# Hybrid decoder step on one core: gate units before attention-branch units, low parts of y in pairs, first state-space branch unit by halves

## The chip, the cores and the metric

One Trainium2 chip, one of its cores. The metric is the device time of one execution in microseconds (us). Every time below comes from the runs of the kernel before or from one profiled execution of it.

## What is computed

One layer of a decoder, for 512 prompt rows and 8 sample rows (together R = 520 columns once the input is transposed). The input is RMS-normalised and multiplied by one large matrix `w_in`. Two branches work on the result: a state-space branch (convolution, chunked scan, gated group norm, giving y with 2048 channels) and an attention branch (three head groups merged into o with 512 channels). Cut to what the change touches, the end of the layer is:

```python
y = yg.reshape(b, t, D_SSD) * ssd_norm_w          # state-space result, 2048 channels
br_ssd = y @ w_ssd_br                             # items "bs"
br_att = o @ w_att_br                             # items "ba"
mix = sigmoid(g_ssd) * br_ssd + sigmoid(g_att) * br_att   # g_ssd: items "gs", g_att: items "ga"
out = x + mix @ w_out                             # items "wo"
```

For the 8 sample rows the state-space branch is one recurrence step: each of 16 units reads a state of 128 x 8 x 128 numbers from memory, forms its share of y from it, scales it by a decay, adds an outer product and stores it again.

## The kernel before, in words

**Numbers.** Every matrix product is made in three passes of a rounded 32-bit type: each operand is split into a high part (H) and a low part (L), and wH·xH, wH·xL and wL·xH are added up in a PSUM bank. ScalarE (ACT) casts to the high part (L1136), VectorE (DVE) subtracts to get the low part (L1511 for weights, L1925 and L1928 for y, L1932 for mix).

**Items and units.** The weights come in 63 items, in the order of `weight_items`; each fills one of two slots of `w_raw`, `wH`, `wL`. SyncE (SP) issues the load of item i once item i-2 is split (L955), ACT casts it once the products of item i-2 are done (L1177), DVE then subtracts. A unit is one block of 128 output channels: a unit of gs or ga has 48 matmuls of 260 columns (8 input tiles, 3 products, 2 halves of the columns), a unit of ba 24, a unit of bs 96 (16 input tiles). gs and ga have 4 items of 2 units each, ba has 2 items of 4 units, bs has 8 items of 1 unit. Units take two pairs of PSUM banks in turn (`cm_bank`), so a unit can start only when the unit two before it has been read out: gs and ga are read by ACT (tanh, L1272), ba and bs by DVE (L1622), wo by DVE (L1639).

**The plan.** `plan()` (L95) writes one list of steps, and each engine walks the same list and does its own part of each step, strictly in order. After the scan of the prompt rows the list `rest` (L220 to L223) has 19 beats, one unit each, with the recurrence of the sample rows laid beside it:

- `sread` u (beat u, u = 0 to 15): DVE waits for the state (L1894), multiplies it with a spread copy of C in a PSUM bank (L1898, twice) and sums (L1905). GpSimd (POOL) forms the outer product (L1116), adds it to the decayed state (L1121) and issues the store (L1123).
- `sdecay` u (beat u+1): ACT scales the state by its decay, 8 instructions (L1429), once DVE has read it (L1426).
- `sload` u (beat u+2): SP waits until the slot's last store has landed (L1000) and issues the next load (L1001). There are 5 slots. SP's queue also holds the weight loads, and behind each of these, up to that of the first bs item, a copy of at most 2 MB from an input cache to an output cache (L949).
- `sgroup` g: TensorE (PE) spreads B and C of a group over the partitions, 32 small matmuls (L920); the C banks are free again only when DVE has read the group's fourth unit (L1902). `sbcopy` g: ACT copies B out of PSUM (L1420), which the outer products wait for (L1113).
- `parts` u: ACT casts unit u of y to yH (L1436), DVE subtracts to yL (L1925). yH lies where the input xH lay, so the first cast waits for the last ga unit (L1434).
- `sfinal` 0 to 2 (beats of the last three ba units): the sample rows' y, its norm and scale. PE's part is a small sum over channels (L927). `sampleparts` splits the sample columns of y.

In the order before, the beats are gs 2 (second unit), gs 3, ga 0, ga 1, ba 0, ga 2, ga 3, ba 1. The parts come four per beat in the last four beats in which the list has room for them, beats 14 to 17 (after the last ga unit and the first three ba 1 units). The first bs unit walks the 16 input tiles in order, three products at each, both halves of the columns side by side, and waits for the low part of each tile and for the sample columns' low part ahead of its first matmul (L610 to L613).

Of the kernel before, what the change touches and what calls it, by code (L numbers as in the profile page):

```python
# [25 lines left out]
P = 128  # L26
# [4 lines left out]
HALF = R // 2  # L31
# [5 lines left out]
UNITS = DSSD // P  # L37
# [24 lines left out]
def weight_items():  # L62

    items = [("rm", g, s, half) for g in range(NG) for s in "qkv" for half in range(2)]
    items += [("za", 0), ("za", 1), ("dt", 0)]
    for g in range(GROUPS):
        items.append(("bc", g))
        for j in range(2 * g, 2 * g + 2):
            items += [("x", j), ("z", j)]
    items += [("gs", j) for j in range(4)]  # L70
    for j in range(2):
        items += [("ga", 2 * j), ("ga", 2 * j + 1), ("ba", j)]
    items += [("bs", j) for j in range(KD)]
    items += [("wo", j) for j in range(4)]
    return items
# [19 lines left out]
def plan():  # L95


    out = [("squares",), ("split", 0), ("init",)]
# [15 lines left out]
    for g in range(NG):  # L114
# [13 lines left out]
        else:  # L128
            beside = []
            for unit in range(2):  # L130
                za_uses.append(proj("za", 0, unit=unit))
                _, i, units = out.pop()
# [26 lines left out]
    n, piece = B * NG, pieces()  # L159
# [27 lines left out]
    for g in range(GROUPS):  # L187
        u = PER_GROUP * g
# [29 lines left out]
    use = proj("gs", 2, unit=0)  # L218
    out += [("sprep",), ("sgroup", 0), use]
    rest = [("gs", 2, 1), ("gs", 3, 0), ("gs", 3, 1)]  # L220
    for j in range(2):
        rest += [("ga", 2 * j + half, unit) for half in range(2) for unit in range(2)]
        rest += [("ba", j, unit) for unit in range(4)]  # L223
    for beat, (kind, j, unit) in enumerate(rest):
        use = proj(kind, j, unit=unit)
        if beat < UNITS:
            if beat and beat % PER_GROUP == 0:
                out.append(("sgroup", beat // PER_GROUP))
            out.append(("sread", beat))
        if beat % PER_GROUP == 1 and beat < UNITS:  # L230
            out.append(("sbcopy", beat // PER_GROUP))
        if 0 < beat <= UNITS:
            out.append(("sdecay", beat - 1))
        if SLOTS_S <= beat - 2 < UNITS:
            out.append(("sload", beat - 2))
        if kind == "ba" and j == 1 and unit > 0:
            out.append(("sfinal", unit - 1))
        out.append(use)
        left = len(rest) - 1 - beat
        if left <= 4:  # L240
            out += [("parts", u) for u in range(4 * (4 - left), 4 * (5 - left)) if u < UNITS]
    out += [("sload", UNITS - 1)] if len(rest) - 2 < UNITS else []
    out.append(("sampleparts",))
    for j in range(KD):
# [74 lines left out]
def hybrid_kernel(nc, xT, wpack, params, consts, sel_in, state_conv, ssm_in, caches,  # L319
                  y_out, tail_out, ssmp_out, kvp_out, ssms_out, kvs_out):  # L320
    ctx = ExitStack()
    with ctx:
# [11 lines left out]
        wH = sb("wH", [P, 2, SLOT], F32R)  # L334
        wL = sb("wL", [P, 2, SLOT], F32R)
# [138 lines left out]
        yL = nc.alloc_sbuf_tensor_at("yL", [P, UNITS, R], F32R, offset=base)  # L474
        yH = nc.alloc_sbuf_tensor_at("yH", [P, UNITS, R], F32R, offset=xH_at)
# [30 lines left out]
        S = {n: sem("s_" + n) for n in names}  # L506
        ends = {}
# [11 lines left out]
        def cm_bank(i, s, hf):  # L519
            if ITEMS[i] == ("za", 0):  # L520

                return banks[((2, 3), (5, 7))[s][hf]]
            return banks[2 * (CMU[i, s] % 2) + hf]

        def wslot(w, i):
            k, n = SHAPES.get(ITEMS[i][0], (KD, 2 * P))
            return w[:, i % 2, 0:k * n].rearrange("p (k n) -> p k n", k=k)
# [36 lines left out]
        def _(pe):  # L564
# [12 lines left out]
            def proj_rows(i, g, s, half):  # L577
# [17 lines left out]
                        mm.then_inc(S["half_item_used"], 1)  # L595
                ends[i] = (banks[NT].filled, banks[NT].uses["rm", g, s, NT]) if half else (S["half_item_used"], i // 2 + 1)

            def proj_cols(i, units, tile, kind, j):

                srcH, srcL = {"bs": (yH, yL), "ba": (oH, oL), "wo": (mH, mL)}.get(kind, (xH, xL))  # L600
                nk = SHAPES.get(kind, (KD,))[0]
                if kind == "ba":
                    pe.wait_ge(S["o_low_ready"], HP)
                for s in units:
                    bk = [cm_bank(i, s, hf) for hf in range(2)]
                    for hf in range(2):
                        if tile in (None, 0):
                            bk[hf].take(pe, ("cm", i, s, hf))
                    for k in range(nk) if tile is None else (tile,):
                        if kind == "bs" and j == 0:  # L610
                            pe.wait_ge(S["y_low_ready"], k + 1)
                            if k == 0:
                                pe.wait_ge(S["sample_y_low_ready"], 1)  # L613
                        if kind == "wo" and j == 0 and s == 0:
                            pe.wait_ge(S["mix_low_ready"], k + 1)
                        for n, (w, x) in enumerate(((wH, srcH), (wH, srcL), (wL, srcH))):
                            for hf in range(2):
                                mm = pe.matmul(bk[hf].tile[:, 0:HALF], wslot(w, i)[:, k, s * P:(s + 1) * P],  # L618
                                               x[:, k, hf * HALF:(hf + 1) * HALF],
                                               start=(k == 0 and n == 0), stop=(k == nk - 1 and n == 2))  # L620
                                if k == nk - 1 and n == 2:
                                    mm.then_inc(bk[hf].filled, 1)
                ends[i] = (bk[1].filled, bk[1].uses["cm", i, s, 1])

            for step in PLAN:
                op, a = step[0], step[1:]
# [2 lines left out]
                elif op == "init":  # L629
# [3 lines left out]
                    for hf in range(2):  # L633
                        banks[hf].take(pe, ("ms", hf))
                        pe.matmul(banks[hf].tile[:, 0:HALF], ones[:, :], xsq[:, 0, hf * HALF:(hf + 1) * HALF],
                                  start=True, stop=True).then_inc(banks[hf].filled, 1)
                elif op == "proj":
                    i = a[0]
# [6 lines left out]
                elif op == "rowtile":  # L645

                    g, t, kk = a
                    i = ITEM_AT["rm", g, "q", kk // 4]
                    pe.wait_ge(S["weight_low_ready"], i + 1)
                    bk = row_bank(g, "q", t)  # L650
                    if kk == 0:
                        bk.take(pe, ("rm", g, "q", t))
                    for n, (x, w) in enumerate(((xH, wH), (xL, wH), (xH, wL))):
                        mm = pe.matmul(bk.tile[:, :], x[:, kk, row_columns(g, t)], wslot(w, i)[:, kk % 4, :],  # L654
                                       start=(kk == 0 and n == 0), stop=(kk == KD - 1 and n == 2))
                    if kk == KD - 1:
                        mm.then_inc(bk.filled, 1)
                elif op == "turn":
# [3 lines left out]
                    for t in range(NT):  # L662
                        pe.wait_ge(S["qk_rows_ready"], qk_count(g, si, t) + 1)
                        bk = banks[5 + turn_c[0] % 3]
                        turn_c[0] += 1
                        bk.take(pe, ("turn", g, si, t))
                        for hp in range(HP):
                            mm = pe.transpose(bk.tile[:, hp * P:(hp + 1) * P], st[:, si, t, hp * P:(hp + 1) * P], ident)
                        mm.then_inc(bk.filled, 1)
                elif op == "scores":  # L670
                    g, h = a
                    n, o, hp = g * SLOTS + h, HD * (h % 2), h // 2
                    if h == 0:
                        pe.wait_ge(S["qk_columns_ready"], 2 * NT * (g + 1))
                    bk = banks[n % 2]
                    bk.take(pe, ("S", n))
                    for t in range(NT):
                        mm = pe.matmul(bk.tile[:, t * P:(t + 1) * P], qT[o:o + HD, hp, t * P:(t + 1) * P],  # L678
                                       kT[o:o + HD, hp, t * P:(t + 1) * P], start=True, stop=True)
                    mm.then_inc(bk.filled, 1)  # L680
                    if g == 0:
                        bk = banks[2 + n % 2]
                        bk.take(pe, ("Sp", n))
                        for t in range(1, NT):
                            mm = pe.matmul(bk.tile[:, (t - 1) * P:t * P], qT[o:o + HD, hp, t * P:(t + 1) * P],
                                           kT[o:o + HD, hp, (t - 1) * P:t * P], start=True, stop=True)
                        mm.then_inc(bk.filled, 1)
                elif op == "probs":
                    g, h = a
                    n = g * SLOTS + h  # L690
                    pe.wait_ge(S["probs_ready"], n + 1)
                    banks[4].take(pe, ("T", n))
                    for t in range(NT):
                        mm = pe.transpose(banks[4].tile[:, t * P:(t + 1) * P], Sx[:, n % 2, t, :], ident)
# [6 lines left out]
                elif op == "values":  # L701
# [7 lines left out]
                    bk = banks[6]  # L709
# [1334 lines left out]
```

## Time and profile before

| | us |
|---|---|
| median of 3 runs | 1187.37 |
| lowest and highest of the 3 | 1184.84, 1188.95 |
| the profiled execution, its own time | 1187.57 |
| its span, first to last instruction | 1185.8 |
| PE busy | 1097.8 (93%) |
| DVE busy | 656.7 (55%) |
| ACT busy | 499.4 (42%) |
| POOL busy | 219.8 (19%) |
| mean granted TensorE clock | 0.94 |

The span is the profiled execution from its first to its last instruction; 1.8 us of its own time lie around it. A share of the busy time is an average over the whole span. The granted clock is 1.00 at 2.4 GHz and 0.50 at 1.2 GHz.

### The profile page before, as it was taken

Reading aid. Unit: us, or ns where it says so; the run is one execution under the profiler, and the core shown is the slowest. Engines: PE = TensorE matmul, PEld = TensorE weight load, DVE = VectorE, ACT = ScalarE, POOL = GpSimd, SP = SyncE. Lnnn points to the kernel's source line nnn. Section 1 sums busy time; section 2 is a strip of 40 time slices with the busy share of each in tenths; the row PEclk is TensorE's granted clock in tenths of the full one; section 3 lists DMA queues with packets and bytes.
Section 4 is the critical chain, followed back from the end, with each engine's and each line's share of the span. In section 5 each row is a group of like instructions: output and inputs, shape, how many; then the busy total and the mean of one; then the engine's idle time right before and its main releaser. Section 6 shows DMA issues by size and latency. Waiting matters only on the chain.

```text
span 1185.8 us, 19650 instructions
## 1 busy us (share of the span) xinstructions
PE 1097.8 (93%) x7838; PEld 1010.2 (85%) x7838; DVE 656.7 (55%) x936; ACT 499.4 (42%) x1130; POOL 219.8 (19%) x209
## 2 busy tenths in 40 slices
PE   4999989999999989895999999999998999689998
PEld 3887779977988779775999899898998999689998
DVE  6663527622462347237677677776764466834342
ACT  5334533345333544102554645656445566612210
POOL 0330003400231000000211220221120589500000
PEclk9998899989999899756999999999999999789999
DMA  8546102580242047145056246254446899432221
GB/s 348 213 169 276 55 1 116 213 329 1 107 168 81 1 151 246 58 152 232 1 219 235 109 162 254 110 218 163 182 175 273 343 360 343 155 144 80 100 98 46
DMA packets 29819, 198.14 MB, mean 167 GB/s; under 512 B 4104, under 2 KB 6280, under 8 KB 20224
## 3 DMA queue, kind: packets, MB, share of 16 engines
q1 hardware_dynamic: 25712, 183.35, 40.5%
q0 software_dynamic: 4016, 13.54, 3.0%
q8 instruction: 62, 1.02, 0.3%
q14 instruction: 29, 0.24, 0.1%
HBM read 180.16 MB, written 104.70 MB: 240 GB/s over the span
## 4 chain that ended last, share of the span: by engine, by line
PE 73%; DVE 11%; ACT 7%; issue 4%; DMA 2%; POOL 2%; SPq 0%; DVEq 0%; ACTq 0%; POOLq 0%
PE bank L618 36%; PE bank L590 16%; DVE cacc L1575 2%; PE bank L813 2%; PE bank L715 2%; ACT wH L1136 2%; PE bank L678 2%; PE bank L767 2%; POOL t L1080 2%; PE bank L884 1%; PE bank L654 1%; DVE wL L1511 1%; DMA slot<-in_state_ssm 1%; PE bank L902 1%; PE bank L876 1%
## 5 line engine op out<-in xcount | busy, mean ns | idle before, releaser
L1511 DVE TENSOR_TENSOR wL<-w_raw,wH 128x2048 fp32r<-128x2048 f32 (+1 forms) x63 | 145.0, 2302 | 155.0 <-ACT wH L1136 152.9
L618 PE MATMUL bank<-xH,wH 128*128 128x260 f32 x976 | 207.9, 294 | 8.1 <-DVEq L1455 6.9
L618 PE MATMUL bank<-xH,wL 128*128 128x260 f32 x976 | 198.1, 285 | 0.0
L618 PE MATMUL bank<-xL,wH 128*128 128x260 f32 x976 | 197.8, 284 | 0.0
L1136 ACT CAST wH<-w_raw 128x2048 fp32r<-128x2048 f32 (+1 forms) x63 | 119.2, 1892 | 136.2 <-PE bank L618 84.8
L618 PEld LDWEIGHTS bank<-xH,wH 128*128 128x128 f32 x976 | 152.0, 191 | 18.8 <-issue 16.6
L618 PEld LDWEIGHTS bank<-xH,wL 128*128 128x128 f32 x976 | 152.0, 190 | 0.0
L618 PEld LDWEIGHTS bank<-xL,wH 128*128 128x128 f32 x976 | 152.0, 190 | 0.0
L590 PE MATMUL bank<-wH,xH 128*128 128x512 f32 x336 | 136.7, 407 | 10.0 <-DVE xL L1490 6.0
L590 PE MATMUL bank<-wH,xL 128*128 128x512 f32 x336 | 134.6, 401 | 0.0
L590 PE MATMUL bank<-wL,xH 128*128 128x512 f32 x336 | 134.6, 401 | 0.0
L590 PEld LDWEIGHTS bank<-wH,xH 128*128 128x128 f32 x336 | 84.0, 250 | 21.2 <-issue 7.0
L1080 POOL TENSOR_TENSOR t<-qn,ropeB 128x256 f32<-128x256 f32 (+1 forms) x60 | 56.0, 951 | 246.4 <-DVE qn L1539 246.3
L590 PEld LDWEIGHTS bank<-wL,xH 128*128 128x128 f32 x336 | 84.1, 250 | 7.8
L590 PEld LDWEIGHTS bank<-wH,xL 128*128 128x128 f32 x336 | 84.3, 251 | 7.4
L1575 DVE SCALAR_TENSOR_TENSOR cacc<-buf,wcv,cacc 128x544 f32<-128x544 f32 x72 | 56.5, 784 | 17.3 <-ACT cacc L1251 15.1
L1294 ACT ACTIVATE Sx<-Sx,nm 128x128 f32<-128x128 f32 x96 | 37.6, 392 | 57.9 <-DVE nm L1669 57.8
L1381 ACT ACTIVATE Lb<-bank,nac 128x128 f32<-128x128 f32 x128 | 36.7, 369 | 47.1 <-PE bank L862 44.3
L1104 POOL TENSOR_TENSOR Eb<-Eb,CT 128x512 f32<-128x512 f32 x32 | 54.0, 1707 | 11.7 <-ACT Eb L1372 11.7
L618 PE MATMUL bank<-yH,wH 128*128 128x260 f32 x256 | 52.6, 287 | 3.5 <-DVE yL L1928 3.5
L618 PE MATMUL bank<-yL,wH 128*128 128x260 f32 x256 | 52.5, 287 | 0.0
L618 PE MATMUL bank<-yH,wL 128*128 128x260 f32 x256 | 52.2, 285 | 0.0
(285 smaller groups left out, 1916.9 us busy)
## 6 DMA issues: line engine op xcount, KB each, us to landing
w_raw<-in_weights SPq DMA_DIRECT2D x62, 1024.0 KB, 5.3
out_kvs<-in_cache SPq DMA_DIRECT2D x16, 2044.0 KB, 10.2
ring<-in_cache SPq DMA_DIRECT2D x48, 256.0 KB, 3.2
slot<-in_state_ssm SPq DMA_DIRECT2D x16, 512.0 KB, 5.9
out_ssm_s<-slot POOLq DMA_DIRECT2D x16, 512.0 KB, 6.0
out_kvs<-in_cache SPq DMA_DIRECT2D x8, 508.0 KB, 8.8
out_kvp<-st POOLq DMA_DIRECT2D x9, 256.0 KB, 2.3
out_kvp<-vv POOLq DMA_DIRECT2D x9, 256.0 KB, 4.6
```

The costliest lines, as they stand in the source:

```text
L590: mm = pe.matmul(bk.tile[:, :], a[:, kk, cols], wslot(b, i)[:, k, :], start=(kk == 0 and n == 0), stop=(kk == KD - 1 and n == 2))
L618: mm = pe.matmul(bk[hf].tile[:, 0:HALF], wslot(w, i)[:, k, s * P:(s + 1) * P], x[:, k, hf * HALF:(hf + 1) * HALF], start=(k == 0 and n == ...
L678: mm = pe.matmul(bk.tile[:, t * P:(t + 1) * P], qT[o:o + HD, hp, t * P:(t + 1) * P], kT[o:o + HD, hp, t * P:(t + 1) * P], start=True, stop ...
L715: mm = pe.matmul(out, vv[:, t, h * HD:(h + 1) * HD], PT[:, n % 2, t, :], start=(t == 0), stop=True, skip_group_check=True)
L767: mm = pe.matmul(banks[6].tile[:, c:c + B + 1:B], KT[:, n % 2, hp, :], qd[:, q0, :], start=True, stop=True, skip_group_check=True)
L1080: ins = nc.gpsimd.tensor_tensor(o[:, :, x, :], v[:, :, 1 - x, :], rb, ALU.mult)
L1104: nc.gpsimd.tensor_tensor(Eb[:, u % 2, e, :], Eb[:, u % 2, e, :], CT[:, 0:T], ALU.mult).then_inc(S["scaled_c_ready"], 1)
L1136: return nc.scalar.copy(out, in_)
L1294: ins = A(Sx[:, n % 2, t, :], Sx[:, n % 2, t, :], ACT.Exp, bias=nm[:, n % 2, t:t + 1], accum_out=lst[:, g, t, h:h + 1])
L1381: ins = A(Lb[:, e, c, :], banks[5 + e].tile[:, c * P:(c + 1) * P], ACT.Exp, bias=nac[:, c, n:n + 1])
L1511: TT(wL[:, i % 2, 0:k * n], raw[:, i % 2, 0:k * n], wH[:, i % 2, 0:k * n].bitcast(F32), ALU.subtract)\
L1575: ins = STT(out=cacc[:, :], in0=bb[:, w:w + CONV], scalar=wcv[:, cu, w:w + 1], in1=cacc[:, :], op0=ALU.mult, op1=ALU.add)
```

## The change

The four ga items now come before the two ba items, in the list of weights and in the beats: gs 2, gs 3, ga 0 to ga 3 (11 beats), then ba 0 and ba 1 (8 beats). The parts of y come two per beat, after beats 10 to 17. `sread`, `sdecay`, `sload` and `sgroup` keep the numbers of their beats, the splits and loads of the weights follow the items. The first bs unit is computed by halves of the columns: first the second half (prompt columns alone), then the first (which has the sample columns); within a half wH·yH over all 16 tiles, wL·yH over all 16, and last wH·yL. It waits for the high parts with the first product and for the low parts with the last, and for the sample columns only in its second half.

```diff
--- before.py
+++ after.py
@@ -68,8 +68,8 @@
         for j in range(2 * g, 2 * g + 2):
             items += [("x", j), ("z", j)]
     items += [("gs", j) for j in range(4)]
-    for j in range(2):
-        items += [("ga", 2 * j), ("ga", 2 * j + 1), ("ba", j)]
+    items += [("ga", j) for j in range(4)]
+    items += [("ba", j) for j in range(2)]
     items += [("bs", j) for j in range(KD)]
     items += [("wo", j) for j in range(4)]
     return items
@@ -218,9 +218,8 @@
     use = proj("gs", 2, unit=0)
     out += [("sprep",), ("sgroup", 0), use]
     rest = [("gs", 2, 1), ("gs", 3, 0), ("gs", 3, 1)]
-    for j in range(2):
-        rest += [("ga", 2 * j + half, unit) for half in range(2) for unit in range(2)]
-        rest += [("ba", j, unit) for unit in range(4)]
+    rest += [("ga", j, unit) for j in range(4) for unit in range(2)]
+    rest += [("ba", j, unit) for j in range(2) for unit in range(4)]
     for beat, (kind, j, unit) in enumerate(rest):
         use = proj(kind, j, unit=unit)
         if beat < UNITS:
@@ -237,8 +236,8 @@
             out.append(("sfinal", unit - 1))
         out.append(use)
         left = len(rest) - 1 - beat
-        if left <= 4:
-            out += [("parts", u) for u in range(4 * (4 - left), 4 * (5 - left)) if u < UNITS]
+        if 0 < left <= 8:
+            out += [("parts", u) for u in range(2 * (8 - left), 2 * (9 - left))]
     out += [("sload", UNITS - 1)] if len(rest) - 2 < UNITS else []
     out.append(("sampleparts",))
     for j in range(KD):
@@ -595,6 +594,20 @@
                         mm.then_inc(S["half_item_used"], 1)
                 ends[i] = (banks[NT].filled, banks[NT].uses["rm", g, s, NT]) if half else (S["half_item_used"], i // 2 + 1)
 
+            def first_branch_unit(i, bk):
+
+                for hf in (1, 0):
+                    bk[hf].take(pe, ("cm", i, 0, hf))
+                    for n, (w, x) in enumerate(((wH, yH), (wL, yH), (wH, yL))):
+                        if hf == 0:
+                            pe.wait_ge(S["sample_y_low_ready"] if n == 2 else S["sample_y_high_ready"], 1)
+                        for k in range(UNITS):
+                            if hf == 1:
+                                pe.wait_ge(S["y_low_ready"] if n == 2 else S["y_high_ready"], k + 1)
+                            mm = pe.matmul(bk[hf].tile[:, 0:HALF], wslot(w, i)[:, k, 0:P], x[:, k, hf * HALF:(hf + 1) * HALF],
+                                           start=(n == 0 and k == 0), stop=(n == 2 and k == UNITS - 1))
+                    mm.then_inc(bk[hf].filled, 1)
+
             def proj_cols(i, units, tile, kind, j):
 
                 srcH, srcL = {"bs": (yH, yL), "ba": (oH, oL), "wo": (mH, mL)}.get(kind, (xH, xL))
@@ -603,14 +616,13 @@
                     pe.wait_ge(S["o_low_ready"], HP)
                 for s in units:
                     bk = [cm_bank(i, s, hf) for hf in range(2)]
+                    if kind == "bs" and j == 0:
+                        first_branch_unit(i, bk)
+                        continue
                     for hf in range(2):
                         if tile in (None, 0):
                             bk[hf].take(pe, ("cm", i, s, hf))
                     for k in range(nk) if tile is None else (tile,):
-                        if kind == "bs" and j == 0:
-                            pe.wait_ge(S["y_low_ready"], k + 1)
-                            if k == 0:
-                                pe.wait_ge(S["sample_y_low_ready"], 1)
                         if kind == "wo" and j == 0 and s == 0:
                             pe.wait_ge(S["mix_low_ready"], k + 1)
                         for n, (w, x) in enumerate(((wH, srcH), (wH, srcL), (wL, srcH))):
@@ -620,7 +632,8 @@
                                                start=(k == 0 and n == 0), stop=(k == nk - 1 and n == 2))
                                 if k == nk - 1 and n == 2:
                                     mm.then_inc(bk[hf].filled, 1)
-                ends[i] = (bk[1].filled, bk[1].uses["cm", i, s, 1])
+                last = 0 if kind == "bs" and j == 0 else 1
+                ends[i] = (bk[last].filled, bk[last].uses["cm", i, s, last])
 
             for step in PLAN:
                 op, a = step[0], step[1:]
```

## Rows read from the trace of the kernel before

**Rows 1.** The page: granted TensorE clock in 40 slices, in tenths

```profile
PEclk9998899989999899756999999999999999789999
```

**Rows 2.** Busy by stretch: length; PE, PEld, DVE, ACT, POOL; clock; DMA share; GB/s

```profile
982.50:1010.95 28.45, 27.14 (x226) 26.96 (x227) 19.56 (x20) 17.28 (x44) 26.55 (x15) 1.00 0.97 356
1010.95:1041.45 30.50, 16.67 (x104) 16.09 (x103) 26.08 (x38) 19.08 (x40) 14.92 (x9) 0.75 0.34 120
1041.45:1055.45 14.00, 14.00 (x97) 14.00 (x98) 2.29 (x1) 0.65 (x1) 0.00 (x0) 0.81 0.53 209
1055.45:1067.00 11.55, 11.55 (x99) 11.55 (x98) 3.84 (x4) 2.44 (x2) 0.00 (x0) 1.00 0.25 92
```

**Rows 3.** The chain that ended last: start, length, what

```profile
954.12 11.52 PE bank L618 x96
...
1041.45 140.52 PE bank L618 x1151
```

**Rows 4.** DVE's instructions in order of time, 1013 to 1033: start, busy, what

```profile
1013.19 5.19 DVE L1925 TENSOR_TENSOR yL<-ygn,yH 128x512 fp32r<-128x512 f32 x4 [2.48 <-ACT yH L1136]
...
1020.51 1.27 DVE L1898 TENSOR_TENSOR sc<-slot,bank 128x512 f32<-128x512 f32 x2
1022.02 1.22 DVE L1905 TENSOR_REDUCE y<-sc 128x8 f32<-128x1024 f32 x1 [0.24 <-DVE sc L1898]
...
1024.77 5.40 DVE L1925 TENSOR_TENSOR yL<-ygn,yH 128x512 fp32r<-128x512 f32 x4
...
1032.24 0.99 DVE L1622 SCALAR_TENSOR_TENSOR mix<-mix,bank 128x260 f32<-128x260 f32 x2
1033.38 2.50 DVE L1925 TENSOR_TENSOR yL<-ygn,yH 128x512 fp32r<-128x512 f32 x4
```

**Rows 5.** POOL's instructions in order of time, 1014 to 1026

```profile
1014.72 1.90 POOL L1116 TENSOR_TENSOR outer<-Bsp,XD 128x1024 f32<-128x1024 f32 x1
1018.97 3.83 POOL L1121 TENSOR_TENSOR slot<-slot,outer 128x1024 f32<-128x1024 f32 x1 [2.35 <-ACT slot L1429]
...
1023.71 1.90 POOL L1116 TENSOR_TENSOR outer<-Bsp,XD 128x1024 f32<-128x1024 f32 x1
1025.69 2.72 POOL L1121 TENSOR_TENSOR slot<-slot,outer 128x1024 f32<-128x1024 f32 x1
```

**Rows 6.** PE's waits in order of time; in brackets the idle time before

```profile
972.84 3.84 PE L920 MATMUL bank<-con,BCS 128*128 128x128 f32 x32 [1.44 <-DVEq L1455]
...
1024.83 0.77 PE L618 MATMUL bank<-oH,wH 128*128 128x260 f32 x2 [8.14 <-DVEq L1455]
...
1032.38 1.20 PE L927 MATMUL bank<-yt,mean_g 128*128 128x32 f32 x8 [2.21 <-DVE yt L1916]
...
1041.45 0.77 PE L618 MATMUL bank<-yH,wH 128*128 128x260 f32 x2 [3.48 <-DVE yL L1928]
```

**Rows 7.** One state on its way, unit 5: read (DVE), decay (ACT), add (POOL)

```profile
960.22 1.28 DVE L1898 TENSOR_TENSOR sc<-slot,bank 128x512 f32<-128x512 f32 x2 [3.58 <-DMA slot<-in_state_ssm]
...
961.54 2.47 ACT L1429 ACTIVATE slot<-slot,dsb 128x128 f32<-128x128 f32 x8 [0.68 <-DVE sc L1898]
...
964.15 2.40 POOL L1121 TENSOR_TENSOR slot<-slot,outer 128x1024 f32<-128x1024 f32 x1 [0.46 <-ACT slot L1429]
```

**Rows 8.** State loads: SP's issues of units 9 and 11, DVE's read of 11

```profile
965.31 0.33 SPq L1001 DMA_DIRECT2D slot<-in_state_ssm  x1
...
979.62 0.43 SPq L1001 DMA_DIRECT2D slot<-in_state_ssm  x1
...
994.15 1.29 DVE L1898 TENSOR_TENSOR sc<-slot,bank 128x512 f32<-128x512 f32 x2 [4.83 <-DMA slot<-in_state_ssm]
```

**Rows 9.** Two short stretches after a wait of PE, columns as in rows 2

```profile
1032.40:1036.40 4.00, 4.00 (x22) 4.00 (x23) 3.56 (x8) 2.59 (x6) 0.00 (x0) 0.60 0.00 0
...
1041.40:1046.80 5.40, 5.35 (x25) 5.38 (x26) 2.29 (x1) 0.69 (x1) 0.00 (x0) 0.50 0.83 342
```

**Rows 10.** Row-major products alone (L590, 512 columns, one bank): length, PE, PEld, clock

```profile
60.00:64.00 4.00, 4.00 (x19) 3.08 (x18) 1.00 0.25 33
```

## The prediction, made before the changed kernel was run

> **What bounds the kernel now.** The page comes first: TensorE (PE) is busy for 93% of the span, and its clock is at 0.9 or more in most slices; one low pair (0.7, 0.8) stands alone in the last third [rows 1]. So the kernel is bound by PE's work, except in a few stretches. The busy time by stretch finds the one that the change touches: from 1010.95 (last ga unit done) to 1041.45 (first bs unit begins) PE is busy for 16.7 of 30.5 us, at a mean clock of 0.75, while VectorE (DVE) is busy for 26.1; before and after it PE is at 95 to 100% [rows 2]. PE's own rows name the waits there: 8.14, 2.21 and 3.48 us, all ended by DVE [rows 6]. After each the clock is at its lower level, 1.2 GHz, for a while [rows 9]: the first bs unit takes 14.0 us, the next 11.55 [rows 2]. From 1041.45 on the chain is PE alone to the last outputs, 140.5 us [rows 3].
>
> PE's bare work from 965.65 to the first bs unit is 4 ga units and 8 ba units. Two ga units take 11.52 us at full clock [rows 3], a ba unit has half the matmuls, 2.9, so 46 us in all, and two spreads at 3.6 to 3.8 [rows 6] make it 54. It takes 75.8 now. 21 us, and the 2.5 us of slow clock in the first bs unit, are the most that any order can give back. What it does give depends on DVE, so I walk DVE's queue through the new order.
>
> **Up to the last ga unit.** Nothing changes before 965.65; the items that change places are equally large. Then PE runs ga 2 (to 977.2), a spread (to 980.8) and ga 3, which ends at 992.3 instead of 1010.95. DVE reads no ga unit, so the four read-outs of ba 0 (0.99 each, 1.15 with the gap) move behind this point. The states behind it move too. POOL's unit 8 waits for a B spread made after ga 2, about 3 us later than now. On SP, the load of ga 3's successor now stands ahead of the state load of unit 9, which goes out at about 972.6 instead of 965.3, behind 1 MB of weights and a 2 MB copy. Unit 11 stood so before: issued at 979.62, read at 994.15, 14.5 us [rows 8]. Unit 9 then lands between 984 and 987; DVE's reads of 9 and 10 are done by about 992, ahead of the parts, so I take 0 and keep 2 us as the bound.
>
> **From there, DVE.** The first part starts 2.2 us after the last ga unit, as now (1010.95 to 1013.19) [rows 2, 4]: 994.5. Until DVE has read out the third unit of ba 1, which frees the banks that the first bs unit needs, it has to do:
> - 14 parts of y at 0.62 (four take 2.50 undisturbed) [rows 4]: 8.8
> - 5 state reads at 2.6 (1.27 + 1.22 and gaps) [rows 4]: 13.0
> - 7 read-outs of ba units at 1.15: 8.1
> - 2 weight splits at 2.2: 4.4
> - the sample rows' seven small operations, 1030.17 to 1032.24 [rows 4]: 2.1
>
> Together 36.4 us, to 1030.9. That would be a gain of about 8 us if nothing else came. But parts also wait for POOL.
>
> **The waits behind POOL.** The first two groups of four parts take 5.19 and 5.40 us, the undisturbed one 2.50 [rows 4]. POOL's rows explain the 2.7 us: at 1024.77 the first part waits for the outer product that ends at 1025.61; the add that stands ready behind it (1025.69, 2.72 instead of 2.40) gets its turn next, and the second part waits for its end at 1028.41 [rows 4, 5]. The other way round, the add of 1018.97 took 3.83 because DVE was splitting weights [rows 5]. So when both queues want to go, they take turns, one instruction each. State reads and read-outs have a PSUM operand or are sums, and show no such waits.
>
> The Trainium skill (SBUF — State Buffer, section on its two separate sides) says that the pair of ports is locked for a whole instruction by whichever started first, which fits these rows; it does not say who goes next when two wait, and by it alone both this forecast and the first rival below would stand.
>
> In the new order this falls badly. A unit's decay starts when the reading multiplications end and takes 2.47; the add follows 3.93 us after the read began (960.22 to 964.15) [rows 7]. DVE meanwhile sums and reads a ba unit out, and reaches its first part at 3.7 us. The part starts, the add arrives 0.2 us later, takes the next turn for 2.40, and the second part of the pair waits. This repeats, since every step hangs on the same read. A beat is then 2.6 + 1.15 + 0.6 + 2.4 + 0.6 = 7.35 us, for PE's 2.9 us of work. Pairs 2 to 5 lose 2.4 each, 9.6; the first pair waits for the outer product of unit 10, 1.1; the second meets outer product and add of unit 10 and 11, about 4.1. Sum 14.8: 1030.9 becomes 1045.7. Groups of four lost 5.3 us in all; pairs lose almost three times that. The bounds for these waits are 0 (1030.9) and 2.7 for each of seven pairs, 18.9 (1049.8).
>
> **TensorE at the end.** Its third ba 1 unit can run from 1036.3, the small sum at 1042.1, the last ba unit from 1043.3 (read-out of the second) to 1046.2. The first bs unit starts at 1046.2. This is where the halves and the low parts last help: the last two parts (1.3 us), the sample rows' scaling, one read-out and the sample columns' split, 4.6 us on DVE between the third read-out and 1041.45 now, are needed only 3.8 and 5.8 us into the unit. Its 96 matmuls now go 48 in a row into one bank instead of to two in turn. The row-major products do that already, 19 of 512 columns in 4 us, 0.21 each at full clock [rows 10], fewer us per column than the 0.12 for 260 here; so I cost the new order at nothing. PE has then worked almost without a break since 1036.3, so I take full clock: 11.5 us, end at 1057.7. Now it ends at 1055.45. The rest, 130.4 us, hangs on PE and moves as a block. The split of the second bs item is at DVE by 1053, in time. PE also waits 2.4 us ahead of the third spread, for DVE's read of unit 11; with the lower clock that may bring it costs nothing, as DVE is the later one by then.
>
> **Sum.** +2.3 us on the profiled execution's 1187.6: 1189.9. The median of the runs is 0.2 below that execution, so I say 1189.7. A measurement of this kernel can tell about 0.3%, 3.6 us, from no change.
>
> **Rivals.**
> *Faster: DVE keeps its turn through a pair.* If the add comes too late to get in (0.2 us decide), both parts pass and the add follows beside the next read. A beat is then set by POOL: outer 1.9, add 2.4, store issue 0.6 and gaps, 5.3 us. Four beats at 2.05 less and 2.2 of the second pair: the bs unit starts at 1035.8 and ends, by its clock, between 1047.3 and 1049.8: 5.6 to 8.1 us less than now, 1179.3 to 1181.8. For it: the two groups of rows 4 lost only one POOL instruction each beyond the first. Against it: at 1025.69 the waiting add did get in between two parts. Chance 0.27.
> *Slower: TensorE stays at the lower clock.* In the ba beats it works 2.9 us and waits for 4.4, and now such waits leave it at 0.50 to 0.60 for the next 4 to 5 us [rows 9]. It decides if the clock is still low at 1043: the last ba unit then takes 5.2 instead of 2.9 (+2.3), and the bs unit 14.0 instead of 11.5 as now [rows 2] (+2.5): +7.1 in all, 1194.5. For it: 4 us of work from 1032.40 did not bring the clock back, and here short breaks lie between. Against it: 5.4 us did after 1041.40. Chance 0.13.
> The Trainium skill (TensorE: Matmul & The Clock Gate, section on HAM oscillation) describes this case, short bursts between waits that find the array slowed each time; the trace agrees for the three waits of rows 6.
> *Late states.* If unit 9 or a later load lands after 988, the reads push the parts back one for one: +2 to +4, 1192 to 1194. Chance 0.05.
>
> **Numbers.** The forecast's own case has 0.55, with an own range of 1186 to 1193.5: the walk has some forty steps, and a third of that case lies above +3.6. Faster: most of the first rival, 0.25, and 0.03 of the forecast's case. Slower: the clock, 0.13, late states 0.03, and 0.18 of the forecast's case. The same: 0.38. The range reaches from the middle of the faster rival, 1180.5, to the slower one, 1194.5.
>
> **What would show it.** Right: the last ga unit ends near 992; the ba beats are 7 to 7.5 us apart on DVE, with one part of each pair at about 3 us; the yL group's sum rises from 15.6 to about 24; PE's longest waits are inside the ba units; the first bs unit starts near 1046, takes 11.5, and its wait is ended by a read-out (L1622), no longer by L1928. Wrong: beats of 5.3 us and parts at 0.69 (first rival); a clock under 0.9 within the bs unit (second); waits of L1898 for state loads after 992 (third).

## The result and the profile after

| | before | changed |
|---|---|---|
| median of 17 runs each, us | 1187.24 | 1190.34 |
| lowest and highest | 1183.27, 1190.92 | 1187.19, 1193.07 |
| ratio to before, 95% interval | | 1.0027 (1.0014 to 1.0040) |
| profiled execution, span | 1185.8 | 1191.0 |

The changed kernel is 3.1 us slower, a little less than the 0.3% that I had set as the limit of what can be told from no change, but the interval excludes 1. The forecast was 1189.7. One execution of a kernel below (e7) was a slow one, 1223.97 us at a mean granted clock of 0.91, and it is left out of its figures.

The profiled execution of the changed kernel took 1192.84 us, 2.5 us above its own median. Part of its longer span lies before the change: the first product of the sample rows' preparation (L907 before, L920 now), where nothing has changed yet, starts 3.45 us later. Single executions of one kernel differ by this much. So that execution is compared with the one before by the distance from this point.

PE, first product of the sample rows' preparation, kernel before:

```profile
915.03 0.64 PE L907 MATMUL bank<-cbp,ones 128*128 128x32 f32 x2 [3.26 <-DVE cbp L1884]
```

The same in the changed kernel:

```profile
918.48 0.64 PE L920 MATMUL bank<-cbp,ones 128*128 128x32 f32 x2 [3.25 <-DVE cbp L1897]
```

The first bs unit's read-out begins when it is done. DVE, kernel before:

```profile
1055.59 1.00 DVE L1622 SCALAR_TENSOR_TENSOR gS<-gS,bank 128x260 f32<-128x260 f32 x2 [11.17 <-PE bank L618]
```

The changed kernel:

```profile
1060.95 0.99 DVE L1635 SCALAR_TENSOR_TENSOR gS<-gS,bank 128x260 f32<-128x260 f32 x2 [6.13 <-PE bank L607]
```

From the one point to the other it is 140.56 us before and 142.47 now: 1.9 us more. The forecast had +2.3 for the end of the first bs unit, with nothing changed before it. After it both run alike (130.2 and 130.05 us to the end of the span).

Busy time by stretch in the changed kernel, from the last ga unit to the first bs unit and that unit alone (columns as in rows 2):

```profile
994.45:1049.36 54.91, 37.92 (x236) 36.69 (x236) 49.70 (x54) 30.30 (x73) 31.99 (x20) 0.78 0.45 163
1049.36:1060.83 11.47, 11.47 (x99) 11.47 (x98) 4.30 (x7) 2.11 (x2) 0.00 (x0) 1.00 0.76 274
```

[rows 2] had 30.5 us with DVE busy for 26.1, and 14.0 us at a clock of 0.81. Now the stretch, which holds four ba units more, takes 54.9 us, DVE is busy for 49.7 of them, and the bs unit takes 11.47 at full clock. DVE's queue between the two, two beats of it:

```profile
1009.82 1.27 DVE L1911 TENSOR_TENSOR sc<-slot,bank 128x512 f32<-128x512 f32 x2
...
1012.37 0.99 DVE L1635 SCALAR_TENSOR_TENSOR mix<-mix,bank 128x260 f32<-128x260 f32 x2
1013.51 3.47 DVE L1938 TENSOR_TENSOR yL<-ygn,yH 128x512 fp32r<-128x512 f32 x2
1016.91 1.27 DVE L1911 TENSOR_TENSOR sc<-slot,bank 128x512 f32<-128x512 f32 x2
...
1020.61 3.49 DVE L1938 TENSOR_TENSOR yL<-ygn,yH 128x512 fp32r<-128x512 f32 x2
1024.02 1.27 DVE L1911 TENSOR_TENSOR sc<-slot,bank 128x512 f32<-128x512 f32 x2
```

Beats are 7.1 us apart (1009.82, 1016.91, 1024.02) and a pair takes 3.47 to 3.49 instead of 1.29. Taken singly, the two parts of each of these pairs last 0.69 and 2.86 to 2.88 us, the short one first.

POOL, same stretch:

```profile
1013.71 2.73 POOL L1134 TENSOR_TENSOR slot<-slot,outer 128x1024 f32<-128x1024 f32 x1 [1.55 <-ACT slot L1442]
...
1020.80 2.75 POOL L1134 TENSOR_TENSOR slot<-slot,outer 128x1024 f32<-128x1024 f32 x1 [1.55 <-ACT slot L1442]
```

Each add arrives 0.2 us after a pair has begun, waits 0.35 us for its first part (2.73 instead of 2.40) and goes ahead of the second. That is the pattern of [rows 4, 5], in three beats running. In the next beat the add began at 1039.43, 0.02 us ahead of the pair, and the first part waited for it (2.91), the second did not (0.68). PE's waits, which [rows 6] had at 8.14, 2.21 and 3.48, now stand ahead of the ba units and of the spread between them. Four are of 2.2 to 2.5 us, and one is of 7.10, ahead of the third ba 1 unit; all five are ended by DVE:

```profile
1002.68 5.46 PE L933 MATMUL bank<-con,BCS 128*128 128x128 f32 x32 [2.24 <-DVEq L1468]
1013.57 0.48 PE L630 MATMUL bank<-oH,wH 128*128 128x260 f32 x2 [2.54 <-DVEq L1468]
1020.66 0.56 PE L630 MATMUL bank<-oH,wH 128*128 128x260 f32 x2 [2.45 <-DVEq L1468]
1027.78 0.77 PE L630 MATMUL bank<-oH,wH 128*128 128x260 f32 x2 [2.47 <-DVEq L1468]
1039.51 0.77 PE L630 MATMUL bank<-oH,wH 128*128 128x260 f32 x2 [7.10 <-DVEq L1468]
1045.17 1.08 PE L940 MATMUL bank<-yt,mean_g 128*128 128x32 f32 x8 [0.19 <-DVE yt L1929]
```

The long one (1032.41 to 1039.51) waits for a read-out that stands on DVE behind the second weight split, which took 4.50 us instead of 2.28 (below). The first bs unit follows the last ba unit without a wait.

### The profile page after: what moved, and what is told of

The parts are those of the page before. It is cut to its first block, busy times and chain, and to the rows that moved or that the text cites. A ratio compares the mean times of both kernels' runs of the same rounds, so it can differ in the third digit from the quotient of the medians.

```text
span 1191.0 us, 19650 instructions
## 1 busy us (share of the span) xinstructions
PE 1103.0 (93%) x7838; PEld 1015.4 (85%) x7838; DVE 664.9 (56%) x936; ACT 498.2 (42%) x1130; POOL 217.8 (18%) x209
## 4 chain that ended last, share of the span: by engine, by line
PE 74%; DVE 12%; ACT 7%; issue 4%; POOL 2%; DMA 1%; SPq 0%; DVEq 0%; ACTq 0%
PE bank L630 36%; PE bank L589 16%; PE bank L728 2%; DVE cacc L1588 2%; PE bank L826 2%; PE bank L691 2%; DVE wL L1524 2%; ACT wH L1149 2%; PE bank L780 2%; POOL t L1093 2%; DVE yL L1938 1%; PE bank L897 1%; PE bank L667 1%; PE bank L915 1%; PE bank L889 1%
## 5 line engine op out<-in xcount | busy, mean ns | idle before, releaser
L630 PEld LDWEIGHTS bank<-xH,wH 128*128 128x128 f32 x976 | 152.8, 192 | 18.2 <-issue 15.6
L1442 ACT ACTIVATE slot<-slot,dsb 128x128 f32<-128x128 f32 x128 | 39.2, 388 | 18.4 <-DVE sc L1911 17.9
L630 PE MATMUL bank<-yL,wH 128*128 128x260 f32 x224 | 45.1, 282 | 0.0
L630 PE MATMUL bank<-yH,wH 128*128 128x260 f32 x224 | 45.0, 282 | 0.0
```

The lines of the kernel that those rows point to most:

```text
L1442: ins = A(st_u[:, b, :], st_u[:, b, :], ACT.Copy, scale=dsb[:, u, b:b + 1])
```

## The experiments

Times are medians, ratios are to the kernel before on the same chip, with their 95% intervals. "Distance" is the one used above, from the first product of the sample rows' preparation to the first bs unit's read-out, from each kernel's profiled execution. "yL sum" is the time of the 16 parts on DVE. The kernel before had medians of 1187.47 beside e1 to e4, 1187.69 beside e5 and e6 and 1185.72 beside e7 and e8, so those two are compared with the others by ratio and distance, not by their medians.

| kernel | median us | ratio to before | distance us | yL sum us |
|---|---|---|---|---|
| before | 1187.24 | 1 | 140.56 | 15.6 |
| changed | 1190.34 | 1.0027 (1.0014 to 1.0040) | 142.47 | 23.7 |
| e1, changed without the halves | 1193.38 | 1.0051 (1.0034 to 1.0069) | 147.84 | 23.8 |
| e2, before with the halves | 1182.37 | 0.9961 (0.9946 to 0.9976) | 134.50 | 15.3 |
| e3, changed, parts in fours | 1187.22 | 0.9997 (0.9977 to 1.0018) | 140.06 | 18.9 |
| e4, changed, a pair in one instruction | 1184.59 | 0.9973 (0.9957 to 0.9989) | 137.24 | 17.1 |
| e5, changed without POOL's add | 1176.89 | 0.9912 (0.9882 to 0.9942) | 131.75 | 10.3 |
| e6, changed, parts ahead of read-out | 1188.61 | 1.0003 (0.9985 to 1.0021) | 142.31 | 19.7 |
| e7, e2 with fours in one instruction | 1179.69 | 0.9955 (0.9934 to 0.9975) | 134.89 | 11.4 |
| e8, e3 with fours in one instruction | 1181.69 | 0.9958 (0.9943 to 0.9973) | 135.33 | 9.6 |

**e1: the halves taken out of the changed kernel.**

```diff
-                    if kind == "bs" and j == 0:
-                        first_branch_unit(i, bk)
-                        continue
...
+                        if kind == "bs" and j == 0:
+                            pe.wait_ge(S["y_low_ready"], k + 1)
+                            if k == 0:
+                                pe.wait_ge(S["sample_y_low_ready"], 1)
```

> The changed kernel with the first bs unit computed as before (tile by tile, both halves of the columns, after the low parts and the sample columns' low part). Theory (DVE's queue sets when the first bs unit starts; the halves only take its last pieces off that chain): the unit starts after the sample columns' split, about 2.4 us later than the 1049.4 of the changed kernel's trace, and after that wait the lower clock costs up to 2.5 us more: 1192.7 to 1195.2. Rival (the halves hide nothing, since the last parts and the sample rows are done anyway by the time the last ba unit is): the same as the changed kernel, 1190.3 within 1.

Measured 1193.38, in the expected range. PE again waits for the sample columns' split, and the unit then takes 13.2 us at a mean clock of 0.87 (the second row below, columns as in rows 2) instead of 11.47:

```profile
1046.69 0.48 PE L617 MATMUL bank<-yH,wH 128*128 128x260 f32 x2 [2.47 <-DVE yL L1927]
```

```profile
1046.70:1059.90 13.20, 13.20 (x98) 13.20 (x98) 2.29 (x1) 0.64 (x1) 0.00 (x0) 0.87 0.58 224
```

The profiled distance says 5.4 us for the halves, the medians 3.0, with intervals of the two ratios that overlap a little. The new order and the pairs alone are 6 us slower than before.

**e2: the halves alone, in the kernel before.** The edit is the changed kernel's `first_branch_unit` and its call, with the items, the beats and the parts left as they were:

```diff
+                    if kind == "bs" and j == 0:
+                        first_branch_unit(i, bk)
+                        continue
...
-                        if kind == "bs" and j == 0:
-                            pe.wait_ge(S["y_low_ready"], k + 1)
...
+                last = 0 if kind == "bs" and j == 0 else 1
```

> The kernel before with the first bs unit by halves alone: order of the items and the four parts per beat as before. Theory (the halves gain, the new order and the pairs lose): the unit starts when the last ba unit is done, 1038.0 instead of 1041.45, and at full clock, so it ends about 5.9 us earlier: 1181.4 against 1187.3, faster than both kernels. Rival (the halves only help where DVE is as late as in the new order): 1185 to 1187.

Measured 1182.37, ratio 0.9961: faster than both kernels. PE's first bs matmuls follow the last ba unit without a wait:

```profile
1037.80 2.07 PE L608 MATMUL bank<-yH,wH 128*128 128x260 f32 x16
```

It was 1041.45 before, after a wait of 3.48 [rows 6], and the read-out now begins at 1049.55 instead of 1055.59. The gain is the 3.65 us of the start and 2.4 us of clock. So of the change, one part gains about 5 us and the other loses about 8 us from there (1182.4 to 1190.3).

**e3: the changed kernel with the parts four per beat.**

```diff
-        if 0 < left <= 8:
-            out += [("parts", u) for u in range(2 * (8 - left), 2 * (9 - left))]
+        if left <= 4:
+            out += [("parts", u) for u in range(4 * (4 - left), 4 * (5 - left)) if u < UNITS]
```

> The changed kernel with the parts of y four per beat in beats 14 to 17, as before; order of the items and halves as changed. Theory (each pair of yL instructions is split by a POOL add, seven pairs; groups of four meet fewer POOL instructions): the three first groups wait some 5 to 6 us in all, not 14 to 15, and the first bs unit starts 8 us earlier; a late state load for unit 13 may take 2 back: 1181 to 1184. Rival (a yL instruction waits as long wherever it stands): 1189 to 1191.

Measured 1187.22. Better than the pairs by 3 us in the medians and 2.4 in the distance (the intervals of the two ratios overlap a little), but not the 1181 to 1184 that were expected. DVE's rows show where I was wrong:

```profile
1012.39 1.00 DVE L1635 SCALAR_TENSOR_TENSOR mix<-mix,bank 128x260 f32<-128x260 f32 x2
1013.53 9.57 DVE L1938 TENSOR_TENSOR yL<-ygn,yH 128x512 fp32r<-128x512 f32 x4
1023.03 4.50 DVE L1524 TENSOR_TENSOR wL<-w_raw,wH 128x2048 fp32r<-128x2048 f32 x1
```

The first group takes 9.57 us (its four parts 1.19, 2.89, 2.90 and 2.82), the weight split behind it 4.50. Without parts between them DVE reads the states every 3.8 us, faster than POOL updates them, so POOL comes to the group with units in arrears, and each of the four parts lets one POOL instruction go first (POOL runs two outer products and two adds in that time, from 1012.26 to 1022.56). A group is not cheaper as such: what counts is how many instructions DVE brings while POOL has work waiting.

e3 also tells the two losing parts of the change apart, since it differs from e2 in the order of ga and ba alone. The order costs 5.6 us of distance (134.50 to 140.06; the intervals of the ratios do not overlap), the pairs 2.4 more. In e2 the first group took 4.86 and the split behind it 2.28, in e3 9.57 and 4.50; only the second group is shorter in e3 (4.36 against 5.40).

**e4: the pair as one DVE instruction.**

```diff
-                    dve.wait_ge(S["y_high_ready"], u + 1)
-                    TT(yL[:, u, B:R], ygn[:, u, B:R], yH[:, u, B:R].bitcast(F32), ALU.subtract).then_inc(S["y_low_ready"], 1)
+                    if u % 2 == 1:
+                        v = slice(u - 1, u + 1)
+                        dve.wait_ge(S["y_high_ready"], u + 1)
+                        TT(yL[:, v, B:R], ygn[:, v, B:R], yH[:, v, B:R].bitcast(F32), ALU.subtract).then_inc(S["y_low_ready"], 2)
```

> The changed kernel with the two yL subtractions of a pair as one DVE instruction of 1024 columns. Theory (DVE and POOL take turns by instruction): no POOL instruction can come in between; the add now waits for the 1.2 us instruction, and the next outer product then delays the next pair, a beat of about 6.5 instead of 7.1 us; yL's busy sum falls from 24 to 15 to 19 us: 1186 to 1188. Rival (POOL slows the subtraction by its elements, or the wait is for the cast): yL's sum and the time stay, 1190.3 within 1.

Measured 1184.59, 1.4 us better than the theory's range, and clearly not the rival's 1190.3. The data are the same, the elements are the same, only the chance to go in between is gone:

```profile
1004.76 1.27 DVE L1911 TENSOR_TENSOR sc<-slot,bank 128x512 f32<-128x512 f32 x2
...
1008.53 2.46 DVE L1940 TENSOR_TENSOR yL<-ygn,yH 128x1024 fp32r<-128x1024 f32 x1 [0.22 <-DVE mix L1635]
1010.92 1.27 DVE L1911 TENSOR_TENSOR sc<-slot,bank 128x512 f32<-128x512 f32 x2
...
1014.70 2.43 DVE L1940 TENSOR_TENSOR yL<-ygn,yH 128x1024 fp32r<-128x1024 f32 x1 [0.22 <-DVE mix L1635]
```

A pair takes 2.4 us (1.2 of work, 1.2 of waiting for one outer product), a beat 6.15 us instead of 7.1.

**e5: POOL's add left out.** The stored sample states lack the outer product; no other output depends on it.

```diff
-                    nc.gpsimd.tensor_tensor(st_u[:, :, :], st_u[:, :, :], outer[:, :, :], ALU.add).then_inc(S["sample_state_ready"], 1)
+                    pool.sem_inc(S["sample_state_ready"], 1)
```

> The changed kernel without POOL's add of the outer product to the decayed sample states (the stored sample states lack that term; nothing else reads it). It takes 16 instructions of 2.4 us off POOL and leaves all waits. Theory: the second part of each pair no longer waits for the add; yL's sum falls from 24 to 11 to 14 us, a beat to 5.0, and the first bs unit starts 9 to 12 us earlier: 1178 to 1181. Rival (DVE's own work or the state loads set the pace): 1187 or more.

Measured 1176.89, ratio 0.9912, below the range of 1178 to 1181. The yL sum is 10.3 us, 0.69 each, nothing waited for:

```profile
1004.39 1.29 DVE L1938 TENSOR_TENSOR yL<-ygn,yH 128x512 fp32r<-128x512 f32 x2
1005.61 1.28 DVE L1911 TENSOR_TENSOR sc<-slot,bank 128x512 f32<-128x512 f32 x2
...
1009.31 1.29 DVE L1938 TENSOR_TENSOR yL<-ygn,yH 128x512 fp32r<-128x512 f32 x2
1010.53 1.27 DVE L1911 TENSOR_TENSOR sc<-slot,bank 128x512 f32<-128x512 f32 x2
```

Beats of 4.9 us, as DVE's own work gives. So the waits of the parts behind POOL are worth 11 to 13 us in the changed kernel: 10.7 by the distance, 13.4 by the medians, of which this one is from four executions. DVE's second weight split still takes 4.37 (at 1020.36), with an outer product beside it (1020.66 to 1022.57), so the add has no part in that wait. And the end is PE's here: from 1028.62, the third ba 1 unit, it works without a wait, at the lower clock until about 1031.4. Leaving out the add also frees POOL and makes the stores earlier, so this is an upper bound for the add alone.

**e6: the pair ahead of the ba unit's read-out.**

```diff
-        out.append(use)
+        late = [("parts", u) for u in range(2 * (8 - left), 2 * (9 - left))] if 0 < left <= 8 else []
+        out += late + [use] if kind == "ba" else [use] + late
```

> The changed kernel with each pair of parts ahead of the ba unit's read-out instead of behind it. Theory (it is the phase of the pair against the add that costs): a pair at 2.6 us after the read's start is through at 3.85, just ahead of the add at 3.93; but the next outer product then meets every second pair, so beats alternate between 5.0 and 8.9 us, mean 6.9 against 7.1: 1188 to 1190.5. Rival (any place ahead of the add frees the pairs altogether): beats of 5.3, 1180 to 1182.

Measured 1188.61; the interval of its ratio and that of the changed kernel's overlap, so the time alone does not tell them apart well. The rows do, as the theory had it, for the first four of them: every second pair is free, the others wait twice.

```profile
1004.47 5.66 DVE L1937 TENSOR_TENSOR yL<-ygn,yH 128x512 fp32r<-128x512 f32 x2
1013.83 1.29 DVE L1937 TENSOR_TENSOR yL<-ygn,yH 128x512 fp32r<-128x512 f32 x2
1018.82 4.86 DVE L1937 TENSOR_TENSOR yL<-ygn,yH 128x512 fp32r<-128x512 f32 x2
1027.38 1.29 DVE L1937 TENSOR_TENSOR yL<-ygn,yH 128x512 fp32r<-128x512 f32 x2
```

The yL sum is 4.0 us smaller than in the changed kernel and the distance only 0.2. The first pair began 1.2 us later (from the point where the distance starts), the last one waited 1.86 for its cast, and the first of the sample rows' small operations took 1.32 instead of 0.28. So the yL sum alone does not give the time.

**e7 and e8: each group of four as one instruction, in both orders.** The edit is that of e4 with 4 for 2, once on e2 and once on e3.

```diff
+                    if u % 4 == 3:
+                        v = slice(u - 3, u + 1)
...
+                        TT(yL[:, v, B:R], ygn[:, v, B:R], yH[:, v, B:R].bitcast(F32), ALU.subtract).then_inc(S["y_low_ready"], 4)
```

> The kernel before with the first bs unit by halves, and each group of four yL subtractions as one DVE instruction of 2048 columns. Theory (every DVE instruction on two SBUF operands can wait for one POOL instruction, so fewer of them wait less): the first group takes about 3.0 us (4.9 without the joining), the second 3.3 (5.4), and 4 us of the 1182.4 go: 1177.5 to 1179.5. Rival (the gain is used up by the sample rows' chain or TensorE's clock): 1181 to 1183.

> The changed kernel with groups of four parts, each as one DVE instruction. It differs from the one beside it in the order of ga and ba alone. In the run with single instructions the first group met four POOL instructions (9.6 us) since POOL was behind with its units. Theory: now it meets one, 3 to 4.3 us, the second 3.3: about 6.5 us of the 1187.2 go, 1180 to 1182, so 2 to 3 us slower than the old order, whose ga beats leave POOL the time to keep up. Rival (without the waits the new order is the better one, as it has the parts ready earlier): at or under the old order's time.

Measured 1179.69 and 1181.69, ratios 0.9955 and 0.9958 with intervals that lie almost on each other. For e7 the expected 4 us did not come (e2: 0.9961, so no gain that can be told). The second group does take 2.93 instead of 5.40, but the add that it no longer lets in goes ahead of the next DVE instruction with two SBUF operands, the first of the sample rows' small ones, which takes 2.46 instead of 0.28; and the first group begins only when all four casts are done:

```profile
1011.53 3.87 DVE L1941 TENSOR_TENSOR yL<-ygn,yH 128x2048 fp32r<-128x2048 f32 x1 [3.21 <-ACT yH L1150]
...
1021.86 2.93 DVE L1941 TENSOR_TENSOR yL<-ygn,yH 128x2048 fp32r<-128x2048 f32 x1 [0.57 <-ACT yH L1150]
1024.71 2.46 DVE L1923 TENSOR_TENSOR y<-y,dsb 128x128 f32<-128x128 f32 x1
```

For e8 4.7 us came by the distance and 4.6 by the ratios (0.9997 to 0.9958), of the 6.5 that were expected; its median lies within the expected range, on a chip where the kernel before is 1.75 us faster than beside e3. With few instructions to wait, the two orders of ga and ba cannot be told apart: 134.9 and 135.3 us of distance. Neither my 2 to 3 us in favour of the old order nor the rival's gain for the new one is shown.

## Why the prediction was right

**What bounds the stretch.** DVE's queue, from the last ga unit to the first bs unit. Shown: DVE is busy for 49.7 of 54.9 us, and e5, which takes nothing off DVE's work, gains 11 to 13 us.

**The walk.** Dates of the changed kernel less its 3.45 us of earlier delay, against the walk. Last ga unit done 991.0 (992.3). First read-out of ba 1 over at 1035.85 (1036.3). First bs unit starts at 1045.9 (1046.2) and ends at 1057.4 (1057.7). Every date is within 1.3 us, most within 0.5. Within it three sizes were off and all but cancelled, which is luck. The last ga unit was done 1.3 us earlier. The second pair took 4.68 and the later ones 3.5 (5.3 and 3.65 in the walk), so a beat was 7.1 and not 7.35, 1.5 us less over all. The second weight split took 4.50 and not 2.2. It ended 2.15 us after the outer product below (1033.46 to 1035.61), and a split alone takes 2.28, so it too waited behind POOL; I had counted POOL's waits for the parts but not for this split, where [rows 5] already showed the pair of them in conflict. DVE:

```profile
1031.11 4.50 DVE L1524 TENSOR_TENSOR wL<-w_raw,wH 128x2048 fp32r<-128x2048 f32 x1
```

POOL:

```profile
1030.94 0.59 POOL L1136 DMA_DIRECT2D out_ssm_s<-slot  x1 [0.30 <-POOL slot L1134]
1031.56 1.90 POOL L1129 TENSOR_TENSOR outer<-Bsp,XD 128x1024 f32<-128x1024 f32 x1
```

One sign did not come: the first bs unit's wait was to be ended by a read-out, and it had no wait; PE's own last ba unit was the later one. The 21 us that the prediction gives as the most that an order can return are 22 by its own terms; nothing hangs on it.

**The waits behind POOL.** Right in kind and in size: the yL sum was to rise from 15.6 to about 24 and rose to 23.7. e4 shows that it is turns by instruction and not a slower rate: the same elements in half as many instructions wait 6.6 us less. The Trainium skill (SBUF — State Buffer, section on its two separate sides) gives the lock for a whole instruction, and the trace agrees (adds of 2.73 instead of 2.40, pairs of 3.47 instead of 1.29); it is silent on who is next, and here the waiting POOL instruction was, in the three beats from 1009.82. The weight split does not fit: by its record it was the one that started first, 0.45 us ahead of the outer product and while POOL was issuing a store, and still it waited until the outer product had ended. The traces do not show what held it.

**The halves.** I named them as the part that helps and gave 4.6 us of DVE's work as what they take off the chain. e2 gives them 5 us by itself, 6.1 in the distance: 3.65 of an earlier start, since there the last ba unit becomes the later one, and 2.4 of clock.

**The order and the pairs.** Here the prediction was right in the sum, but gave the pairs more of it than is theirs. It set the pairs' waits (14.8) against the 5.3 that groups of four lost in the old order, and did not ask what they would lose in the new one. That is 8.6 (a yL sum of 18.9 in e3 against 10.3 undisturbed) and 2.2 of the split. So most of the loss comes with the order (e2 to e3, 5.6 us) and the smaller part with the pairs (e3 to the changed kernel, 2.4). With the parts joined the order costs nothing that can be told (e7, e8).

**The rivals.** The faster one (DVE keeps its turn through a pair) has fallen: the pairs of beats 12 to 14 were parted, and that of beat 15 waited as a whole. The slower one, the clock, did not come to count. It did fall to its lower level after PE's waits in the ba beats (0.50 from 1014.2 to 1017.2, from 1027.8 to 1030.9 and from 1039.5 to 1044.4), but was at 1.00 from 1045 on, before the last ba unit began (1046.23). The margin was small: at the lower clock the third ba 1 unit was done at 1044.99, 0.13 us before the sample rows' last operation on DVE (1045.12), which PE had to wait for anyway. Late states did not happen either: unit 9 was read at 988.84, after a wait of 3.16 for its load, and its reads were over before the last ga unit (994.45), as the walk had it.

```profile
1040.00:1045.00 5.00, 4.99 (x24) 4.74 (x22) 4.80 (x9) 1.60 (x2) 2.41 (x2) 0.52 0.27 108
1045.00:1049.00 4.00, 3.83 (x31) 3.77 (x32) 3.41 (x8) 1.55 (x4) 0.00 (x0) 1.00 0.00 0
```

**Left open.** Why a split that starts during a store's issue waits for the outer product behind it. And whether single parts, moved so that they meet POOL's gaps only, would lose nothing in the new order; it was not tried.

## What to carry to other kernels

When DVE's queue sets the end, count its instructions on two SBUF operands, not only their time: each one can wait for a whole GpSimd instruction, so many short ones between the steps of a GpSimd chain cost more than a few long ones, and what one no longer waits for may wait ahead of the next. A reordering that fills TensorE's queue gains nothing where another engine's queue is the later one, and it can cost time (5.6 us of distance from e2 to e3). Before a loss is laid on one part of a change, the parts are to be tried one by one. A consumer that takes its late operands in its last product and its latest columns in its last half (5 us of 1187 here) is worth trying alone, without the reordering that came with it.

## What was not expected of the hardware

Splitting work on DVE into smaller pieces locked it in step with GpSimd: the step that starts a beat on DVE also releases, 3.9 us later, the GpSimd add, so the meeting repeated over three beats, the add 0.19 to 0.20 us behind the pair in each. But the time did not hang on that hit: e6 moved the pairs to another place in the beat and its distance is the changed kernel's within 0.2 us. And in e3 four instructions in a row let four GpSimd instructions through, one each (9.57 us for 2.5 us of work): being first in its own queue with the next one ready gave DVE no second turn. In two cases the POOL instruction that was let through had not even begun by its record: the third part of that group started at 1017.5, the outer product at 1017.90, and the split of the changed kernel at 1031.11, the outer product at 1031.56. Both times POOL was issuing a store just then. In the kernel before, a part that started at 1028.9, during the issue of 1028.71 with no outer product behind it, was not held (0.68 us).
